# Splitting each row gather and scatter of a mixture-of-experts kernel in two, and moving a wait and the routing of the last token tile

## The chip, the cores and the metric

One NeuronCore of one Trainium2 chip runs the whole program. The metric is device time in microseconds (us) of one execution. The kernel before takes 714.67 us, the median of three runs (713.92 to 717.95).

## The reference, cut to what matters

One layer works on 512 tokens of width 1024. A token mixer comes first (one combined projection, four branches, sigmoid gates, an output projection), then a mixture of experts, then a last RMSNorm. What the change touches is the mixture:

```python
g_idx = jnp.argmax(group_probs, axis=-1)                 # 1 of 4 groups
top_p, top_i = lax.top_k(jax.nn.softmax(in_group), 2)    # 2 of its 8 experts
expert_id = g_idx[:, None] * 8 + top_i
for e in range(32):
    hid = jax.nn.silu(t @ w_expert_gate[e]) * (t @ w_expert_up[e])
    out = out + combine[:, e:e + 1] * (hid @ w_expert_down[e])
```

Each token goes to two of 32 experts, so there are 1024 token rows to gather and as many result rows to put back. The weights of all the experts, 96 matrices of 1 MB, are read once. The reference's routing on its own inputs gives the experts 0 to 31 these numbers of tokens:

```
6 30 32 38 12 22 2 4 64 60 45 26 52 49 28 16 35 31 47 33 34 32 49 11 23 34 56 19 25 14 30 65
```

## The kernel before, in words

**Mixer.** TensorE works through eleven slices of the combined projection (the last is `fk`, the keys of the forgetting attention), then through sixteen steps of attention, into which the first gate products are woven by `gates(count)`. Ahead of the first gate products TensorE waits until all six attention slices have been taken out of PSUM (`evacuated`, L1822 and on). `fk` sits in banks 4 and 5; the first 24 gate products write bank 6 and the six branch products behind them write bank 4.

**Output projection and routing.** The output projection runs over two halves of the columns, b = 0 and 1, and four tiles of 128 tokens each (L2008). VectorE adds each result to the residual (`residual`, L1114), TensorE transposes the sum (L1957), ScalarE copies it out of PSUM (L1000), and TensorE forms the router logits (`router_logits`, L1967). VectorE then picks the group and the two experts in a chain of small dependent instructions (`route`), TensorE counts the earlier tokens of each expert (`rank_products`, L1978), and VectorE makes two one-hot matrices: `chosen`, which picks the rows of expert pair 0, and `hot`, which makes the table of slots. `choose_rows` (L2014) multiplies `chosen` with the tokens, so pair 0 needs no gather. Its two PSUM banks are copied out, one by ScalarE (L1020) and one by VectorE (L1442). `first_table` (L2031, L1986) makes the table.

**Expert turns.** Experts are worked in pairs, each with 64 slots: the even expert of a pair has partitions 0 to 63, the odd one 64 to 127. There are 17 turns. Turns 0 to 6 are pairs 0 to 6. Turn 7 (`OVER`) is the fullest expert alone, its tokens over 64 in the second half; turn 8 (`PART`) is its partner alone in the first half. Turns 9 to 15 are pairs 8 to 14, and turn 16 is pair 7, in the place of the pair that was taken apart; the results of turns 15 and 16 stay on the chip and are not scattered. A turn is: gate and up matmuls (L2155), transposes of the next turn's gathered rows `xg` (L2121), transposes of the hidden values (L2164), down matmuls (L2181), then ScalarE and VectorE each copy half of the result to the one buffer `ye` (L1059, L1652), which may be done only when the scatter of the turn before has landed.

**Queues.** GpSimd issues one indirect gather per turn (L726, `xg` from `x2_dram`, rows by `toks`) and one indirect scatter (L733, `ye` to `y_dram`, rows by `slots`). Both have 128 rows; those of turn 8 have 64. An empty slot holds an index that is out of bounds, and its row is not moved. SyncE issues the weights in a fixed order into a ring of 21 units of 1 MB (L521), each as soon as the unit that held its place has been used: a gate unit frees with `g_done`, an up unit with `gu_done`, a down unit with `y_ps`. When the scatters have landed it issues the loads of the result rows of token tile 1 (L600), the last two weight units, and the other result rows. VectorE adds up the rows of tile 1 ahead of the hidden values of the last turn (`gather_results`, L1093), and the last norm follows.

**Places of slots.** `slot_no` says which of an expert's tokens a partition holds. Partition 32a + 4b + d of a half holds the tokens 32a + 8d to 32a + 8d + 7, forwards or backwards over b = 0 to 7.

Of the kernel before, what the change touches and what calls it, by code (L numbers as in the profile page):

```python
# [48 lines left out]
def hybrid_trunk(nc, x, mix_norm_g, w_in, b_forget, conv_a_w, conf_dw_w, conf_dw_b, conf_ln_g,  # L49
                 conf_ln_b, w_branch, w_gate, b_gate, w_out, ffn_norm_g, w_router_group,  # L50
                 w_router_expert, w_expert_gate, w_expert_up, w_expert_down, final_norm_g, out):
    P = 128
# [50 lines left out]
    with main:  # L103
# [182 lines left out]
        toks = sb(moe, "toks", [NPAIR + 1], I32)  # L286
        cw_diag = sb(moe, "cw_diag", [2, P])
# [119 lines left out]
        FIXED = 4  # L407
        LAST = NPAIR
# [14 lines left out]

        def halves(row):

            return row.rearrange("p (b n) -> p b n", b=2)

# [51 lines left out]
        def _(sp_e):  # L479
# [94 lines left out]
            for t in range(NT):  # L574
                sp_e.wait_ge(S["x2_ready"], NT + t + 1)
# [26 lines left out]
            for s in range(2):  # L602
                sp_e.wait_ge(scattered[s], 16 * (NPAIR // 2 - s))
# [16 lines left out]
            with sp_e.If(most > SLOT):  # L620
                sp_e.wait_ge(S["out_done"], 16 * NT)
                with sp_e.Fori(1, PASSES) as c:

                    sp_e.wait_ge(S["y_ps"], c * (2 * NPAIR) + 2)
                    sp_e.wait_ge(S["rank_ready"], NT)
                    for w in range(NPAIR * UPP):
                        if w >= NUP:
                            wait_reuse(c, w)
                        load_unit_no(w, c)
                for s in range(2):  # L630
                    sp_e.wait_ge(scattered[s], 16 * (NPAIR // 2 * PASSES - s))
# [7 lines left out]
        def _(pool):  # L639
# [79 lines left out]
            def rows_of(c, i):  # L719

                return slice(0, SLOT if isinstance(c, int) and i == PART else P)

            def gather(c, i, s):

                n, p = rows_of(c, i), column(c, i)
                pool.indirect_dma_start(out=xg[n, s, :], out_offset=None, in_=x2_dram[:, :],  # L726
                                        in_offset=bass.IndirectOffsetOnAxis(ap=toks[n, p], axis=0),
                                        bounds_check=last_token, oob_is_err=False).then_inc(g_full[s], 16)

            def scatter(c, i, s):  # L730

                n, p = rows_of(c, i), column(c, i)
                pool.indirect_dma_start(out=y_dram[:, :], out_offset=bass.IndirectOffsetOnAxis(ap=slots[n, p], axis=0),  # L733
                                        in_=ye[n, :], in_offset=None, bounds_check=last_row,
                                        oob_is_err=False).then_inc(scattered[s], 16)

            def expert_pass(c):
# [3 lines left out]
                pool.wait_ge(S["idx_ready"], c + 1)  # L741
# [40 lines left out]
        def _(act):  # L782
# [213 lines left out]
            def router_input(n):  # L996

                b, t = n // NT, n % NT
                act.wait_ge(S["xt2_ps"], n + 1)
                act.activation(xt2[:, t % 2, b * (KC // 2):(b + 1) * (KC // 2), :], bank[4 + n % 2][:, :].rearrange("p (c s) -> p c s", s=P),  # L1000
                               ACT.Copy).then_inc(S["moved_a"], 1)

            def token_squares(n):

                b, t = n // NT, n % NT
                act.wait_ge(S["x2_ready"], n + 1)
# [12 lines left out]
            act.wait_ge(S["routed_ps"], NT + 1)  # L1019
            act.activation(xg[:, 0, 0:T], bank[0][:, :], ACT.Copy).then_inc(S["moved_a"], 1)  # L1020
# [8 lines left out]
            def expert_pass(c):  # L1029

                first = c if isinstance(c, int) else 1
                for i in range(NPAIR + 1 if isinstance(c, int) else NPAIR):
# [19 lines left out]
                    else:  # L1052

                        if not isinstance(c, int):
                            act.wait_ge(scattered[1 - s], c * (NPAIR // 2 * 16) + ((i - 1) // 2 + s) * 16)
                        elif i:
                            act.wait_ge(scattered[1 - s], ((i - 1) // 2 + 1) * 16)
# [31 lines left out]
        def _(dve):  # L1089
# [18 lines left out]
            def residual(t, b):  # L1108
# [4 lines left out]
                half = x2[:, t, b * T:(b + 1) * T]  # L1113
                dve.tensor_tensor(half, half, bank[t][:, :], ALU.add).then_inc(S["x2_ready"], 1)  # L1114
# [251 lines left out]
            def route(t):  # L1366
# [10 lines left out]
                st.link(stt(re[:, 2, :], ro[:, 0, t, :], 2 * FAR, re[:, 0, :], ALU.mult, ALU.add))  # L1377
                yield
                first_max(re[:, 2, :], NE, rs[:, 3, t:t + 1], re[:, 3, :], best)
                st.mark(dve.tensor_scalar(rg[:, 0, t, :], gl, top, None, ALU.subtract))  # L1380
                dve.wait_ge(S["m_ready"], 2 * t)
                stt(rmask[:, t, :], re[:, 3, :], best, ro[:, 0, t, :], ALU.is_equal, ALU.add).then_inc(S["m_ready"], 1)
                dve.tensor_scalar(ro[:, 1, t, :], re[:, 3, :], best, None, ALU.is_equal).then_inc(S["m_ready"], 1)
                dve.wait_ge(S["m_ready"], 2 * t + 2)
                for j in range(2):
                    st.mark(dve.tensor_scalar(rv[:, t, j, :], ro[:, j, t, :], row_no[:, t, j:j + 1], None, ALU.mult))
                yield
# [46 lines left out]
            dve.wait_ge(S["sq_done"], 3 * NT)  # L1434
            dve.reduce_sum(stat[:, 0, :], sq_part[:, :, :], AX.X).then_inc(S["sq2_sum"], 1)
            for part in range(2):
                next(routes[NT - 1])
            choose(NT - 1)
            rank_tokens(NT - 2)
            rank_tokens(NT - 1)  # L1440
            dve.wait_ge(S["routed_ps"], NT + 2)
            dve.tensor_copy(xg[:, 0, T:2 * T], bank[1][:, :]).then_inc(S["hot_ready"], 1)  # L1442

            def slot_columns(n, found):

                table = found[:, 256:256 + NE].rearrange("p (e h) -> p h e", h=2)
                for h in range(2):
                    half = slice(h * SLOT, (h + 1) * SLOT)
                    dve.tensor_scalar(slots[half, 0:NPAIR], table[half, h, :], float(UNUSED), None, ALU.add).then_inc(S["slots_in"], 1)
                dve.wait_ge(S["slots_in"], n)  # L1450
                dve.tensor_scalar(toks[:, 0:NPAIR], slots[:, 0:NPAIR], 1, None, ALU.arith_shift_right).then_inc(S["idx_ready"], 1)

# [52 lines left out]
            def exchange_columns():  # L1505
# [6 lines left out]
                st.link(dve.tensor_copy(slots[:, FIXED:NPAIR], slot_f[:, FIXED:NPAIR]))  # L1512
                one_column(bank[7][:, 256:256 + NE], emask)
# [21 lines left out]
            def overflow_column():  # L1535

                second = slice(SLOT, P)
# [3 lines left out]
                st.link(dve.tensor_scalar(slots[second, NPAIR:NPAIR + 1], rs[second, 13, 0:1], float(UNUSED), None, ALU.add))  # L1541
# [4 lines left out]
            def first_exponents():  # L1546

                st.link(dve.tensor_tensor(rg[:, 2, :, :], rg[:, 0, :, :], stat[:, 2, :].unsqueeze(2).to_broadcast([P, NT, NG]), ALU.mult))
# [46 lines left out]
            def expert_pass(c):  # L1595
# [5 lines left out]
                if isinstance(c, int):  # L1601
                    dve.wait_ge(S["slot_ps"], 1)
                    slot_columns(2, bank[3])
# [8 lines left out]
                for i in range(turns):  # L1612
# [32 lines left out]
                    else:  # L1645

                        if not isinstance(c, int):
                            dve.wait_ge(scattered[1 - s], c * (NPAIR // 2 * 16) + ((i - 1) // 2 + s) * 16)
                        elif i:
                            dve.wait_ge(scattered[1 - s], ((i - 1) // 2 + 1) * 16)  # L1650
# [32 lines left out]
            with dve.If(most[0] > SLOT):  # L1683
# [20 lines left out]
                with dve.Fori(1, PASSES) as c:  # L1704

                    for s in range(2):
                        dve.wait_ge(scattered[s], c * (NPAIR // 2 * 16) - s * 16)
# [3 lines left out]
                    slot_columns(c * 2 + 2, bank[7])  # L1711
# [12 lines left out]
        def _(pe):  # L1724
# [90 lines left out]
            for name in ("sq", "sk", "sv", "fq", "fk", "fv"):  # L1815
# [55 lines left out]
            gates(PER_TILE)  # L1871
# [77 lines left out]
            def router_transposes(n):  # L1949
# [5 lines left out]
                for c in range(KC // 2):  # L1955
                    d = (b * (KC // 2) + c) * P
                    last = nc.tensor.transpose(bank[4 + n % 2][:, c * P:(c + 1) * P], x2[:, t, d:d + P], ident[:, :])  # L1957
                last.then_inc(S["xt2_ps"], 1)

            def router_logits(n):  # L1960

                b, t = n // NT, n % NT
                pe.wait_ge(S["moved_a"], n + 1)
                if b and t:
                    pe.wait_ge(S["m_ready"], 2 * t - 1)
                for c in range(b * (KC // 2), (b + 1) * (KC // 2)):
                    last = nc.tensor.matmul(bank[6][:, t * NR:(t + 1) * NR], xt2[:, t % 2, c, :], wr[:, c, :],  # L1967
                                            start=c == 0 and t == 0, stop=c == KC - 1, skip_group_check=True)
# [67 lines left out]

            first_table()
# [25 lines left out]
            def table_products(i, k):  # L2063
# [9 lines left out]
                if i == SPILL and k == 0:  # L2073
                    pe.wait_ge(S["hot_ready"], ALL_HITS + 2)
# [38 lines left out]
            def x_transposes(c, i, s, b):  # L2113

                if isinstance(c, int) and i == 0:
                    pe.wait_ge(S["moved_a"], 2 * NT + 1)
                    pe.wait_ge(S["hot_ready"], ALL_HITS + 1)
                elif b == 0:
                    pe.wait_ge(g_full[s], (i + 1) // 2 * 16 if isinstance(c, int) else c * (NPAIR // 2 * 16) + (i // 2 + 1) * 16)
# [5 lines left out]
            def expert_pass(c):  # L2125
# [69 lines left out]
            with pe.If(most > SLOT):  # L2195
                pe.wait_ge(S["rank_ready"], NT)
                with pe.Fori(1, PASSES) as c:
                    pe.wait_ge(S["hot_ready"], c + (ALL_HITS + 2))
# [30 lines left out]
```

## Time and profile before

| | |
|---|---|
| median of three runs | 714.67 us |
| the profiled execution | 714.88 us |
| its span, first to last instruction | 712.9 us |
| around the span | 2.0 us |
| granted TensorE clock, mean | 0.997 |
| TensorE matmul busy | 690.4 us, 97% of the span |
| VectorE, ScalarE, GpSimd busy | 372.7, 254.7, 80.0 us |
| bytes moved by DMA | 164.57 MB, mean 231 GB/s |

The page and the answers of the trace give the time of each instruction, what ended the idle time before it, and how busy the 16 DMA engines of the core were. "DMA share" is the mean busy share of these 16, so a share near 0.5 may be eight engines busy and eight idle. Share and GB/s can differ: an engine whose packets take long is busy and moves little.

### The profile page before, as it was taken

What the parts mean: (1) busy time and instruction counts of PE and PEld (TensorE: products, weight loads), DVE (VectorE), ACT (ScalarE), POOL (GpSimd) and SP (SyncE); (2) the same over time, 40 slices, a digit from 0 to 9 for tenths busy, and PEclk for the clock granted to TensorE, in tenths of its full rate; (3) what the DMA queues carried; (4) which work ended last, traced back from release to release, by engine and by line L of the source; (5) the groups of instructions that cost most, each with busy time, mean ns of one, the idle gap of its engine ahead of it and who ended that gap; (6) DMA issues with size and microseconds to landing.
All of it is one profiled execution on the core that took longest, in us unless ns stands there. A gap on an engine that the chain in (4) does not pass through costs nothing.

```text
span 712.9 us, 10002 instructions
## 1 busy us (share of the span) xinstructions
PE 690.4 (97%) x3923; PEld 507.5 (71%) x3923; DVE 372.7 (52%) x725; ACT 254.7 (36%) x423; POOL 80.0 (11%) x116
## 2 busy tenths in 40 slices
PE   7999999999999999999999999999999999999794
PEld 6888988777777777788888888665555556555442
DVE  5378996667676868656446214852423221212227
ACT  7332134577676777544243211210111111111113
POOL 2000922000000101100003000011111112121000
PEclk9999999999999999999999999999999999999998
DMA  7523144322222111493406699699999999999983
GB/s 241 176 63 116 61 126 147 134 74 75 74 74 68 46 60 53 161 384 114 135 2 236 239 376 348 268 353 394 399 417 421 403 420 419 418 418 418 420 353 130
DMA packets 60360, 164.57 MB, mean 231 GB/s; under 512 B 7866, under 2 KB 39687, under 8 KB 47892
## 3 DMA queue, kind: packets, MB, share of 16 engines
q1 hardware_dynamic: 54820, 151.77, 56.1%
q0 software_dynamic: 5488, 12.11, 4.5%
q8 instruction: 33, 0.54, 0.3%
q14 instruction: 19, 0.16, 0.1%
HBM read 155.68 MB, written 16.00 MB: 241 GB/s over the span
## 4 chain that ended last, share of the span: by engine, by line
PE 90%; DMA 4%; DVE 4%; ACT 1%; issue 1%; SPq 0%; POOLq 0%; DVEq 0%; ACTq 0%
PE psum L1731 31%; PE psum L2155 15%; PE psum L1830 12%; PE psum L2181 8%; PE psum L2008 6%; PE psum L1842 3%; PE psum L2121 2%; DMA ring_e<-y_dram 2%; DVE ring_e L1093 2%; PE psum L1855 1%; PE psum L1884 1%; DMA y_dram<-ye,slots 1%; PE psum L2164 1%; PE psum L1967 1%; PE psum L1919 1%; PE psum L1907 1%
## 5 line engine op out<-in xcount | busy, mean ns | idle before, releaser
L1731 PE MATMUL psum<-xh,wh 128*128 128x512 f32 x256 | 99.9, 390 | 0.8 <-DVE xl L1093 0.8
L1731 PE MATMUL psum<-xl,wh 128*128 128x512 f32 x256 | 99.6, 389 | 0.0
L1731 PE MATMUL psum<-xh,wl 128*128 128x512 f32 x256 | 99.6, 389 | 0.0
L1096 DVE TENSOR_TENSOR wl<-raw,wh 128x1280 fp32r<-128x1280 f32 (+4 forms) x37 | 71.8, 1946 | 24.8 <-ACT wh L789 9.0
L1093 DVE SCALAR_TENSOR_TENSOR hid<-psum,rslot,act_g 128x256 f32<-128x256 f32 x17 | 8.2, 484 | 95.1 <-PE psum L2155 94.6
L1731 PEld LDWEIGHTS psum<-xh,wh 128*128 128x128 f32 x256 | 48.1, 188 | 11.1 <-DVE xl L1093 1.0
L1731 PEld LDWEIGHTS psum<-xh,wl 128*128 128x128 f32 x256 | 48.1, 188 | 9.9
L1731 PEld LDWEIGHTS psum<-xl,wh 128*128 128x128 f32 x256 | 48.1, 188 | 9.8
L1830 PE MATMUL psum<-xh,wh 128*128 128x512 f32 x128 | 51.3, 401 | 1.3 <-DVE k_fl L1093 1.3
L1830 PE MATMUL psum<-xh,wl 128*128 128x512 f32 x128 | 50.1, 391 | 0.0
L1830 PE MATMUL psum<-xl,wh 128*128 128x512 f32 x128 | 49.9, 390 | 0.0
L1093 DVE SCALAR_TENSOR_TENSOR sg<-cu,ch,sg 128x512 f32<-128x512 f32 x60 | 48.8, 886 | 0.0
L2155 PE MATMUL psum<-ring_w,xT 128*64 128x256 f32 x256 | 38.8, 383 | 0.0
L1042 ACT ACTIVATE act_g<-psum,rslot 128x256 f32<-128x256 f32 x17 | 8.1, 474 | 80.2 <-PE psum L2155 60.7
L1044 ACT ACTIVATE hidT<-psum 128x256 f32<-128x256 f32 x17 | 6.5, 384 | 78.4 <-PE psum L2164 78.4
L1652 DVE COPY ye<-psum 128x512 f32<-128x512 f32 x15 | 10.4, 692 | 44.2 <-PE psum L2181 44.2
L733 POOL DMA_INDIRECT y_dram<-ye,slots x15 | 15.1, 1007 | 158.1 <-DVE ye L1652 114.5
L1323 DVE TENSOR_TENSOR gp<-gs,psum 128x512 f32<-128x512 f32 x16 | 11.0, 687 | 36.4 <-PE psum L1731 35.6
L2155 PEld LDWEIGHTS psum<-ring_w,xT 128*64 128x64 f32 x256 | 22.4, 136 | 10.5 <-issue 3.4
L964 ACT ACTIVATE gs<-psum,bg 128x512 f32<-128x512 f32 x16 | 10.9, 687 | 49.8 <-PE psum L1731 49.7
L1830 PEld LDWEIGHTS psum<-xh,wh 128*128 128x128 f32 x128 | 24.1, 188 | 6.2 <-issue 1.7
L1830 PEld LDWEIGHTS psum<-xh,wl 128*128 128x128 f32 x128 | 24.0, 188 | 5.2
(383 smaller groups left out, 1517.1 us busy)
## 6 DMA issues: line engine op xcount, KB each, us to landing
raw<-in_w_gate SPq DMA_DIRECT2D x16, 1024.0 KB, 6.4
raw<-in_w_in SPq DMA_DIRECT2D x9, 1024.0 KB, 5.5
ring_w<-in_w_expert_gate SPq DMA_DIRECT2D x8, 1024.0 KB, 20.4
ring_w<-in_w_expert_up SPq DMA_DIRECT2D x8, 1024.0 KB, 17.1
ring_h<-in_w_expert_down SPq DMA_DIRECT2D x8, 1024.0 KB
ring_h<-in_w_expert_gate SPq DMA_DIRECT2D x6, 1024.0 KB
ring_e<-in_w_expert_down SPq DMA_DIRECT2D x6, 1024.0 KB, 17.7
ring_e<-in_w_expert_gate SPq DMA_DIRECT2D x6, 1024.0 KB, 22.5
```

The lines of the kernel that those rows point to most:

```text
L733: pool.indirect_dma_start(out=y_dram[:, :], out_offset=bass.IndirectOffsetOnAxis(ap=slots[n, p], axis=0), in_=ye[n, :], in_offset=None, bo ...
L964: act.activation(gs[:, m, :], gate_bank(cg, m)[:, :], ACT.Sigmoid, bias=bg[:, d:d + 1]).then_inc(S["gate_mul"], 1)
L1093: return dve.scalar_tensor_tensor(out=out_, in0=a, scalar=s, in1=b, op0=o0, op1=o1)
L1096: return dve.tensor_tensor(dst, src, hi.bitcast(F32), ALU.subtract)
L1323: dve.tensor_tensor(gp[:, m, :], gs[:, m, :], branch_bank(cg, m)[:, :], ALU.mult).then_inc(S["gate_free"], 1)
L1731: last = nc.tensor.matmul(dst, a, b, start=start and n == 0, stop=stop and n == len(seq) - 1)
L1830: last = nc.tensor.matmul(bank[6 + n % 2][:, :], a[:, c, f], b[:, c, :], start=c == 0 and q == 0, stop=c == KC - 1 and q == 2)
L1842: last = nc.tensor.matmul(bank[4 + n % 2][:, :], a[:, j, f], b[g][:, j, :], start=j == 0 and q == 0, stop=j == BJ - 1 and q == 2)
L2008: last = nc.tensor.matmul(bank[t][:, :], x_[:, t, c, :], w_[:, b, c, :], start=c == 0 and m == 0, stop=c == KC - 1 and m == 2)
L2121: last = nc.tensor.transpose(bank[b][:, (k % 4) * P:(k % 4 + 1) * P], xg[:, s, :].rearrange("p (n c) -> p c n", c=KC)[:, k, :], ident[:, :])
L2155: last = nc.tensor.matmul(dst[half, 0:FE], xT[:, k, half], w[h][:, k, :], start=k == 0, stop=k == KC - 1)
L2181: last = nc.tensor.matmul(bank[5 + b][half, :], hidT[:, m, half], w_d[h][:, m, b * T:(b + 1) * T], start=m == 0, stop=m == FE // P - 1)
```

## The change

1. Every gather and every scatter is two: one for partitions 0 to 63 and one for 64 to 127, each with 64 rows. Two new columns, `slots_b` and `toks_b`, hold the indices of the second half in partitions 0 to 63. Semaphore counts double (`HALVES`), less 16 behind turn 8, which has one half only.
2. The order of `slot_no` changes: the eight-token groups k = 0 to 3 sit at d = 0, 2, 3, 1 for a = 0 and at d = 2, 0, 1, 3 for a = 1.
3. The wait for `fk` stands behind the first 24 gate products.
4. The last token tile's second half is added, transposed, copied and multiplied in two parts of 256 columns (`blocks_of`).
5. In `route`, two instructions move from the second part to the first; `rg` is no longer made per tile but once in `first_exponents`; the row values of the last two tiles and the sum of squares come later (`row_values`). `choose_rows(0, 1)` goes behind the last logits.
6. ScalarE copies both banks of pair 0, and `first_table` goes behind the transposes of pair 0.

```diff
+        HALVES = 2 * 16
+        def blocks_of(n):
+            return (slice(0, KC // 4), slice(KC // 4, KC // 2)) if n == 2 * NT - 1 else (slice(0, KC // 2),)
+        def one_less(s, i=PART):
+            return 16 if s == PART % 2 and i >= PART else 0
...
             def gather(c, i, s):
-                n, p = rows_of(c, i), column(c, i)
-                pool.indirect_dma_start(out=xg[n, s, :], out_offset=None, in_=x2_dram[:, :],
-                                        in_offset=bass.IndirectOffsetOnAxis(ap=toks[n, p], axis=0),
+                p = column(c, i)
+                pool.indirect_dma_start(out=xg[first, s, :], out_offset=None, in_=x2_dram[:, :],
+                                        in_offset=bass.IndirectOffsetOnAxis(ap=toks[first, p], axis=0),
                                         bounds_check=last_token, oob_is_err=False).then_inc(g_full[s], 16)
+                if whole(c, i):
+                    pool.indirect_dma_start(out=xg[second, s, :], out_offset=None, in_=x2_dram[:, :],
+                                            in_offset=bass.IndirectOffsetOnAxis(ap=toks_b[first, p], axis=0),
+                                            bounds_check=last_token, oob_is_err=False).then_inc(g_full[s], 16)
...
-                    for d in range(4):
-                        base, step = SLOT // 2 * a + 8 * d, 1
-                        if d % 2:
+                    for k, d in enumerate((2, 0, 1, 3) if a else (0, 2, 3, 1)):
+                        base, step = SLOT // 2 * a + 8 * k, 1
+                        if k % 2:
...
-                dve.tensor_tensor(half, half, bank[t][:, :], ALU.add).then_inc(S["x2_ready"], 1)
+                for part in (slice(0, T // 2), slice(T // 2, T)) if b and t == NT - 1 else (slice(0, T),):
+                    half = x2[:, t, b * T:(b + 1) * T][:, part]
+                    dve.tensor_tensor(half, half, bank[t][:, part], ALU.add).then_inc(S["x2_ready"], 1)
...
             for n in range(2 * NT):
                 router_input(n)
                 token_squares(n)
+            for b in range(2):
+                act.wait_ge(S["routed_ps"], NT + b + 1)
+                act.activation(xg[:, 0, b * T:(b + 1) * T], bank[b][:, :], ACT.Copy).then_inc(S["moved_a"], 1)
...
-            for name in ("sq", "sk", "sv", "fq", "fk", "fv"):
+            for name in ("sq", "sk", "sv", "fq", "fv"):
                 evacuated(pe, name)
...
-            gates(PER_TILE)
+            gates(BEHIND_SCORES)
+            evacuated(pe, "fk")
+            gates(PER_TILE - BEHIND_SCORES)
...
             router_transposes(2 * NT - 1)
-            choose_rows(0, 1)
             rank_products(NT - 2)
             router_logits(2 * NT - 1)
+            choose_rows(0, 1)
...
-            first_table()
...
                 for b in range(2):
                     x_transposes(c, 0, first % 2, b)
+                if isinstance(c, int):
+                    first_table()
```

## Rows read from the trace of the kernel before

**Rows 1.** The chain that ended last (start us, us, what), from turn 13.
```profile
643.51 3.65 PE psum L2181 x16
...
655.70 3.68 PE psum L2181 x16
659.47 0.70 DVE ye L1652
...
660.99 8.79 DMA y_dram<-ye,slots
670.17 14.43 DMA ring_e<-y_dram
684.63 1.30 DVE ring_e L1093
```

**Rows 2.** Stretches of the run, with DMA share and GB/s at the end of each row.
```profile
454.00:690.00 236.00, 228.09 (x1597) 132.85 (x1595) 69.53 (x206) 30.02 (x60) 31.27 (x31) 1.00 1.01 407
468.00:470.00 2.00, 2.00 (x22) 1.61 (x20) 1.77 (x12) 1.26 (x1) 1.10 (x2) 1.00 0.81 264
```

**Rows 3.** Who TensorE waited for, from 655 to 690 us.
```profile
PE psum L2155 <- DMA ring_x<-in_w_expert_up: 1.6, 1, 1.6
```

**Rows 4.** Stretches at the end of the DMA work.
```profile
688.00:689.00 1.00, 1.00 (x6) 0.87 (x7) 0.00 (x0) 0.39 (x1) 0.00 (x0) 1.00 1.05 426
692.00:693.00 1.00, 1.00 (x8) 0.29 (x5) 0.20 (x1) 0.69 (x1) 0.00 (x0) 1.00 0.52 213
689.00:698.00 9.00, 9.00 (x34) 3.94 (x33) 4.17 (x5) 2.66 (x3) 0.00 (x0) 1.00 0.44 178
```

**Rows 5.** DMA queue of the gathers and scatters: packets, MB, share; 505 to 685 us.
```profile
q0 software_dynamic: 3707, 7.09, 10.4%
```

**Rows 6.** The same queue, 1.1 us of turn 7's scatter (579.7), then of turn 8's (591.75).
```profile
q0 software_dynamic: 40, 0.07, 17.5%
...
q0 software_dynamic: 37, 0.12, 27.7%
```

**Rows 7.** Stretches around turn 8's gather, issued at 552.54.
```profile
505.00:557.00 52.00, 51.85 (x382) 29.73 (x380) 14.06 (x39) 5.75 (x12) 8.03 (x8) 1.00 1.02 420
559.00:560.00 1.00, 1.00 (x8) 0.37 (x6) 0.00 (x0) 0.00 (x0) 0.00 (x0) 1.00 1.03 254
560.00:561.00 1.00, 1.00 (x8) 0.35 (x6) 0.00 (x0) 0.42 (x1) 0.00 (x0) 1.00 0.97 332
561.00:562.00 1.00, 1.00 (x8) 0.43 (x6) 0.08 (x1) 0.18 (x1) 0.00 (x0) 1.00 1.01 393
```

**Rows 8.** Instructions in order of time: projection end, routing of the last tile, turn 0.
```profile
138.88 0.47 PE L1830 MATMUL psum<-xh,wh 128*128 128x512 f32 x1 [1.32 <-DVE k_fl L1093]
...
454.94 1.06 PE L1967 MATMUL psum<-wr,xt 128*128 128x36 f32 x8
...
455.84 3.68 PE L2014 MATMUL psum<-x,chosen 128*128 128x512 f32 x8
...
459.58 0.24 PE L1978 MATMUL psum<-rmask,oneb 128*128 128x32 bf16 x3
...
462.59 1.04 PE L1986 MATMUL psum<-rv,hot 128*128 128x32 f32 x8
...
463.52 1.13 PE L2121 MATMUL psum<-ident,xg 128*128 128x128 f32 x8
...
465.16 3.67 PE L2155 MATMUL psum<-ring_z,xT 128*64 128x256 f32 x32 [0.51 <-DVE xT L1463]
```

**Rows 9.** A usual turn: scatter, the two copies waiting for it, its issue to landing.
```profile
612.21 1.00 POOL L733 DMA_INDIRECT y_dram<-ye,slots  x1 [9.87 <-DVE ye L1652]
...
621.16 0.60 ACT L1059 ACTIVATE ye<-psum 128x512 f32<-128x512 f32 x1 [2.10 <-PE psum L2181]
622.88 0.69 DVE L1652 COPY ye<-psum 128x512 f32<-128x512 f32 x1 [3.07 <-PE psum L2181]
...
DMA to landing us min/median/max: 8.5/8.5/8.5
```

More of the change, by code:

```diff
@@ L286, in hybrid_trunk @@
         toks = sb(moe, "toks", [NPAIR + 1], I32)
+        slots_b = sb(moe, "slots_b", [NPAIR + 1], I32)
+        toks_b = sb(moe, "toks_b", [NPAIR + 1], I32)
         cw_diag = sb(moe, "cw_diag", [2, P])
@@ L574, in _ @@
             for t in range(NT):
-                sp_e.wait_ge(S["x2_ready"], NT + t + 1)
+                sp_e.wait_ge(S["x2_ready"], NT + t + 1 if t < NT - 1 else 2 * NT + 1)
                 sp_e.dma_start(x2_dram[t * P:(t + 1) * P, :], x2[:, t, :]).then_inc(S["x2_out"], 16)
@@ L998, in router_input @@
                 b, t = n // NT, n % NT
-                act.wait_ge(S["xt2_ps"], n + 1)
-                act.activation(xt2[:, t % 2, b * (KC // 2):(b + 1) * (KC // 2), :], bank[4 + n % 2][:, :].rearrange("p (c s) -> p c s", s=P),
-                               ACT.Copy).then_inc(S["moved_a"], 1)
+                for k, part in enumerate(blocks_of(n)):
+                    act.wait_ge(S["xt2_ps"], n + k + 1)
+                    act.activation(xt2[:, t % 2, b * (KC // 2):(b + 1) * (KC // 2), :][:, part, :],
+                                   bank[4 + (n + k) % 2][:, :].rearrange("p (c s) -> p c s", s=P)[:, part, :], ACT.Copy).then_inc(S["moved_a"], 1)
             def token_squares(n):
                 b, t = n // NT, n % NT
-                act.wait_ge(S["x2_ready"], n + 1)
+                act.wait_ge(S["x2_ready"], n + 1 if n < 2 * NT - 1 else 2 * NT + 1)
                 if n:
@@ L1438, in _ @@
             choose(NT - 1)
+            for t in (NT - 2, NT - 1):
+                row_values(t)
             rank_tokens(NT - 2)
             rank_tokens(NT - 1)
-            dve.wait_ge(S["routed_ps"], NT + 2)
-            dve.tensor_copy(xg[:, 0, T:2 * T], bank[1][:, :]).then_inc(S["hot_ready"], 1)
+            dve.wait_ge(S["sq_done"], 3 * NT)
+            dve.reduce_sum(stat[:, 0, :], sq_part[:, :, :], AX.X).then_inc(S["sq2_sum"], 1)
             def slot_columns(n, found):
@@ L1512, in exchange_columns @@
                 st.link(dve.tensor_copy(slots[:, FIXED:NPAIR], slot_f[:, FIXED:NPAIR]))
+                st.link(dve.tensor_copy(slot_f[first, :], slots_b[first, 0:NPAIR]))
+                exchanged(moved[first, :], slot_f[first, :], slot_f[first, OVER:OVER + 1], gap[first, :])
+                st.link(dve.tensor_copy(slots_b[first, FIXED:NPAIR], slot_f[first, FIXED:NPAIR]))
+                st.mark(dve.tensor_scalar(toks_b[first, FIXED:NPAIR], slots_b[first, FIXED:NPAIR], 1, None, ALU.arith_shift_right))
                 one_column(bank[7][:, 256:256 + NE], emask)
@@ L1535, in overflow_column @@
             def overflow_column():
-                second = slice(SLOT, P)
+                first, second = slice(0, SLOT), slice(SLOT, P)
                 dve.wait_ge(S["slot_ps"], 3)
@@ L1540, in overflow_column @@
                 one_column(bank[7][:, 256:256 + NE], fmask)
-                st.link(dve.tensor_scalar(slots[second, NPAIR:NPAIR + 1], rs[second, 13, 0:1], float(UNUSED), None, ALU.add))
+                st.mark(dve.tensor_scalar(slots[second, NPAIR:NPAIR + 1], rs[second, 13, 0:1], float(UNUSED), None, ALU.add))
+                st.link(dve.tensor_scalar(slots_b[first, NPAIR:NPAIR + 1], rs[first, 13, 0:1], float(UNUSED), None, ALU.add))
+                st.link(dve.tensor_scalar(toks_b[first, NPAIR:NPAIR + 1], slots_b[first, NPAIR:NPAIR + 1], 1, None, ALU.arith_shift_right))
                 dve.tensor_scalar(toks[:, NPAIR:NPAIR + 1], slots[:, NPAIR:NPAIR + 1], 1, None, ALU.arith_shift_right).then_inc(S["over_ready"], 1)
@@ L1954, in router_transposes @@
                     pe.wait_ge(S["moved_a"], n - 1)
[L1955 to L1958, printed above, removed]
+                for k, part in enumerate(blocks_of(n)):
+                    if k:
+                        pe.wait_ge(S["x2_ready"], n + k + 1)
+                        pe.wait_ge(S["moved_a"], n)
+                    for c in range(KC // 2)[part]:
+                        d = (b * (KC // 2) + c) * P
+                        last = nc.tensor.transpose(bank[4 + (n + k) % 2][:, c * P:(c + 1) * P], x2[:, t, d:d + P], ident[:, :])
+                    last.then_inc(S["xt2_ps"], 1)
             def router_logits(n):
                 b, t = n // NT, n % NT
-                pe.wait_ge(S["moved_a"], n + 1)
                 if b and t:
                     pe.wait_ge(S["m_ready"], 2 * t - 1)
-                for c in range(b * (KC // 2), (b + 1) * (KC // 2)):
-                    last = nc.tensor.matmul(bank[6][:, t * NR:(t + 1) * NR], xt2[:, t % 2, c, :], wr[:, c, :],
-                                            start=c == 0 and t == 0, stop=c == KC - 1, skip_group_check=True)
+                for k, part in enumerate(blocks_of(n)):
+                    pe.wait_ge(S["moved_a"], n + k + 1)
+                    for c in range(b * (KC // 2), (b + 1) * (KC // 2))[part]:
+                        last = nc.tensor.matmul(bank[6][:, t * NR:(t + 1) * NR], xt2[:, t % 2, c, :], wr[:, c, :],
+                                                start=c == 0 and t == 0, stop=c == KC - 1, skip_group_check=True)
                 if b:
```

63 lines of the change are left out of this document (35 added, 28 removed).

## The prediction

> **What bounds the kernel now.** I read the chain of waits first, then the DMA share by stretches, then who TensorE waits for. From 139 us to 459 us TensorE is never idle for long: the one stop by another engine is 1.32 us, ahead of the first gate product, until VectorE has taken `fk` out of PSUM [rows 8]. In the expert turns it is busy too, and this misleads: from 454 to 690 us the DMA engines have a share of 1.01 and move 407 GB/s [rows 2], while a turn eats six units, 6.3 MB, in 655.70 - 643.51 = 12.2 us [rows 1], which would be 516 GB/s. So the ring of 21 units runs empty, slowly, and by turn 15 TensorE waits for weights [rows 3]. The chain says the same: after turn 14 it goes through the last scatter, then 14.43 us of the load of the result rows, then VectorE [rows 1]. The DMA work from 454 us on is a fixed number of bytes, and the end is where it is done plus some 28 us of tail behind 684.63.
>
> **How it ends is the second thing to see.** At 688 us all engines are busy (1.05), at 692 the share is 0.52, and over the 9 us to 698 it is 0.44 [rows 4]. A mean engine is thus done at 689 + 9 x 0.44 = 693.0, the last at 698: some lag the mean by 5 us, and about half of them are late together. [...] In 1.1 us of turn 8's scatter, which has 64 rows and 30 tokens, 0.12 MB went; in as much time of turn 7's, which has 128 rows and its 65 tokens all but one in the first half, 0.07 MB [rows 6]. [...] The first halves hold much more: the even experts have 540 of the 1024 tokens, and turns 7 and 8 put 94 of their 95 in the first half. [...] A row costs an engine 0.104 x 180 us x 16 / (7.09 MB / 4096) = 0.173 us [rows 5]. [...]
>
> **The change part by part.** All in the profiled execution's own time, 714.88 us (712.9 of span and 2.0 around it); it lies 0.2 above the median of the runs.
>
> *The wait for `fk`.* The 1.32 us go. The 24 gate products now ahead of the wait are some 5 us of work (at most 24 x 0.47 [rows 8]) that need only the slices before, and VectorE is through with `fk` 1.3 us in. Nothing late comes next: up to 459 us TensorE has no second stop above 0.3 us. I take -1.3; the bounds are 0 (if ScalarE and VectorE set the pace of the attention steps) and -1.3.
>
> *The last tile's halves and the order of `route`.* Today the logits end at 456.00, four products of `choose_rows` fill TensorE to 459.52, and `rank_products` starts at 459.58 [rows 8], as VectorE's mask arrives. The halves bring the logits forward by some 0.6 us (one part's copy and products in place of two), and `route` gets 0.2 shorter, but `choose_rows(0, 1)`, 3.68 / 4 = 0.9 us, now stands behind the logits. So 455.4 + 5 x 0.86 = 459.7: the products now end last, and VectorE's gain is wasted. +0.1. If I mis-sized this by one such product, it is -0.8 to +0.2.
>
> *`first_table` behind the transposes.* Today it runs in the shadow of the two copies (1.04 us at 462.59, transposes from 463.52 [rows 8]). Then TensorE idles 0.51 us until VectorE has made the first half of `xT`. In the new order the transposes start at the same 463.5, since ScalarE makes both copies and the second one ends at 463.4; they end at 464.6, the table takes 1.3 us, and the gate products start at 465.9, not 465.16. +0.7. Bounds +0.2 and +1.1. Behind it the slots come 0.4 us later, and with two more small instructions the first gather 0.6; its landing has some 3 us to spare. SyncE's first refill waits for the gate products of turn 0 and is as late; the DMA engines are already short of work there (264 GB/s [rows 2]), so the 0.7 counts in full.
>
> *Two DMAs for one.* On GpSimd a turn has four issues of 1.3 us and not two, 5.2 of 12.2 us: nothing else is queued there. The second scatter is issued 1.3 us later. The scatter lands 8.5 us after its issue, at 620.7; ScalarE's copy wants it at 621.16 and VectorE's at 622.88 [rows 9]. ScalarE will be up to 1 us late, which nobody waits for, VectorE is in time. Cost 0, at most 0.5. VectorE's exchange in turn 2 is longer by about six small instructions, 1.2 us; the gather of turn 4 behind it has some 4 us to spare. 0.
>
> *The balance.* [...] It is a gain of 3.3 to 3.8; I take 3.3. [...] Bounds: 0 and -4.6.
>
> The sum: 714.9 - 1.3 + 0.1 + 0.7 - 3.3 = **711.1 us**.
>
> [...] In stretches of 1 us around turn 8's gather, the only gather before that has 64 rows, the rate falls from 420 to 254, 332 and 393 GB/s, at a full share [rows 7]; turn 8's scatter shows no such dip, and in 185 us there is no other. The shortfall is (166 + 88 + 27) KB / 420 GB/s = 0.67 us for 30 rows. [...]
>
> **The rivals.**
>
> *Narrow gathers choke (slower), 0.30.* Every gather becomes two like that of turn 8. The dip costs 0.67 us per 30 rows, and some 880 rows are gathered from turn 3 on: 19.7 us if each half pays in full. The second half follows 1.3 us behind and goes to the other 64 partitions, while the dip lasts 3 us, so about half may be saved: 9.8. The scatter's part of the balance (half of 3.3) stays. 714.9 - 0.5 - 1.6 + 9.8 = 722.6, up to 732 in full. It decides from 0.11 us per 30 rows on, where the loss eats the gain of 3.3 us; against it stands only that it is one event, seen alone and not with its other half beside it.
>
> *The halves don't even out (the change doesn't do what it says), 0.20.* [...] Then only the wait and the table count: 714.9 - 1.3 + 0.8 = 714.4. The same figure comes out if a mild choking, some 3 us, pays for the balance.
>
> **How the numbers follow.** The forecast has a chance of 0.50, with its own range 709.0 to 713.3 (balance by 4.6 and routing by -0.8 on one side, the wait lost on the other). No change that a measurement of this kernel can tell is within 0.5%, or 711.1 to 718.2 us: the forecast lies on its lower edge. So half of its chance is faster, with a little of the second rival: 0.29. The same: 0.25 + 0.16 = 0.41. Slower: 0.30. The range reaches from 709.0 to 724.5, which leaves out the full choking.
>
> **What would show it.** Right: no stop at the first gate product; gate products of turn 0 starting 0.7 us later than the rest of the shift; DMA share falling from 1 to 0 within 3 us, not 9; the rate between 505 and 650 us still near 420. Wrong: that rate at 400 or less with a full share, TensorE waiting for weights from turn 12 or 13 on; or a share near 0.5 for several us at the end as before.

## The result, and the profile after

The changed kernel takes 723.76 us (median of 4 runs, 722.86 to 724.27); the kernel before took 715.28 us beside it. The ratio is 1.0112, with a 95% interval of 1.008 to 1.0145: slower by 8.0 us (5.7 to 10.4), where I had forecast 3.8 us faster. The profiled execution took 722.86 us, its span is 721.1. The time is close to that of my first rival (722.6), to which I had given 0.30. Below, "faster by x us" is a ratio of runs of one session turned into us at 714.5, with its 95% interval in brackets; it can differ from the difference of the two medians by up to 1 us.

Stretches of the changed kernel (start and end, length, busy us of TensorE, its weight loads, VectorE, ScalarE, GpSimd, granted clock, DMA share, GB/s). The first row answers to [rows 2]; the last four are from two neighbouring turns:

```profile
454.00:690.00 236.00, 223.50 (x1540) 128.90 (x1539) 64.99 (x205) 28.87 (x57) 56.56 (x60) 0.99 1.01 386
505.00:685.00 180.00, 169.85 (x1173) 97.42 (x1170) 38.33 (x80) 20.27 (x41) 45.16 (x48) 0.98 1.02 385
522.00:529.00 7.00, 7.00 (x55) 4.26 (x51) 0.00 (x0) 0.47 (x1) 3.76 (x4) 0.93 1.01 413
529.00:535.00 6.00, 6.00 (x28) 3.60 (x27) 0.07 (x1) 0.00 (x0) 0.00 (x0) 0.51 1.02 301
535.00:545.00 10.00, 9.96 (x74) 5.61 (x75) 5.00 (x17) 1.45 (x3) 2.65 (x3) 1.00 1.01 418
545.00:550.00 5.00, 4.47 (x34) 2.68 (x32) 1.77 (x3) 0.38 (x1) 1.20 (x2) 1.00 1.01 420
```

The GpSimd issues whose rows move in those stretches (start, us, operation):

```profile
524.91 0.96 POOL L739 DMA_INDIRECT xg<-x_dram,toks  x1 [0.30 <-issue]
526.17 0.96 POOL L743 DMA_INDIRECT xg<-x_dram,toks_b  x1 [0.30 <-issue]
541.74 0.92 POOL L750 DMA_INDIRECT y_dram<-ye,slots  x1 [14.60 <-DVE ye L1692]
542.96 1.01 POOL L754 DMA_INDIRECT y_dram<-ye,slots_b  x1 [0.31 <-issue]
```

The share of the DMA engines is full in both kernels (1.01 and 1.02): by the share alone nothing has happened. What fell is what they move in that share, from 418 to 385 GB/s over 505 to 685 us. The engines aren't idle, their packets take longer: a packet of the weights' queue took 0.896 x 180 us x 16 / 8537 packets = 302 ns in this stretch, and 0.909 x 180 us x 16 / 9575 = 273 ns in the kernel before. The rate falls in bursts, one per turn, and from 665 to 685 us, behind the last gather (issued at 658.56), it is 415 again. The gathers issued at 524.91 and 526.17 move their rows from 529 to 535 us, and there the rate is 301 (414 in the same stretch of the kernel before). The scatters issued at 541.74 and 542.96 move theirs from 545 to 550 us, and there it is 420. TensorE's clock happens to be low in that one burst (0.51). It isn't the cause: in the split alone (below) the same burst has a clock of 1.00 and 327 GB/s:

```profile
529.00:535.00 6.00, 5.96 (x42) 3.76 (x43) 1.61 (x3) 0.38 (x1) 0.00 (x0) 1.00 1.03 327
```

Who TensorE waited for in the changed kernel (us in total, times, longest), to be held against [rows 3]:

```profile
PE psum L2210 <- DVE hid L1116: 6.5, 11, 1.6
...
PE psum L2201 <- DMA ring_x<-in_w_expert_up: 1.8, 1, 1.8
...
PE psum L2227 <- DMA ring_q<-in_w_expert_down: 0.8, 1, 0.8
PE psum L2201 <- DMA ring_e<-in_w_expert_up: 0.7, 1, 0.7
```

Its waits for `hid`, the hidden values that VectorE makes, have grown too. In the kernel before they were:

```profile
PE psum L2164 <- DVE hid L1093: 2.0, 2, 1.7
```

The chain that ended last, from turn 13 on, which answers to [rows 1]:

```profile
630.40 32.96 DMA ring_q<-in_w_expert_down
663.49 3.67 PE psum L2227 x16
667.25 0.70 DVE ye L1692
...
669.98 8.13 DMA y_dram<-ye,slots_b
678.51 14.27 DMA ring_e<-y_dram
692.80 1.30 DVE ring_e L1116
```

Its first row is what the chain before did not have: a step that waits for a weight unit. The 33 us from issue to landing are not new in themselves, since one unit (`ring_p`, 33.0 us) took as long in the kernel before; new is that the products stand behind it. The last scattered turn's down products, which started at 655.70 [rows 1], start at 663.49.

The end of the DMA work, in stretches of 1 us, which answers to [rows 4]:

```profile
701.00:702.00 1.00, 1.00 (x7) 0.19 (x4) 0.72 (x1) 0.04 (x1) 0.00 (x0) 1.00 1.01 401
702.00:703.00 1.00, 1.00 (x3) 0.52 (x4) 0.32 (x1) 0.98 (x2) 0.00 (x0) 1.00 0.90 360
703.00:704.00 1.00, 1.00 (x3) 0.38 (x2) 1.00 (x2) 0.95 (x1) 0.00 (x0) 1.00 0.73 295
704.00:705.00 1.00, 1.00 (x5) 0.42 (x3) 0.96 (x2) 0.00 (x0) 0.00 (x0) 1.00 0.44 176
705.00:706.00 1.00, 1.00 (x5) 0.67 (x4) 0.96 (x2) 0.00 (x0) 0.00 (x0) 1.00 0.18 74
```

The shares from 701 us on add up to 3.3, so a mean engine is done at 704.3 and the last at 706: the lag is 1.7 us, where it was 5. In this execution the balance came as forecast, and the sum closes: the mean engine is done 704.3 - 693.0 = 11.3 us later, the lag is 3.3 smaller, together 8.0; the span grew by 721.1 - 712.9 = 8.2.

### The profile page after: what moved, and what is told of

Its sections match the earlier page's. It is cut to its first block, busy times and chain, and to the rows that moved or that the text cites. A ratio compares the mean times of both kernels' runs of the same rounds, so it can differ in the third digit from the quotient of the medians.

```text
span 721.1 us, 10044 instructions
## 1 busy us (share of the span) xinstructions
PE 694.0 (96%) x3923; PEld 509.4 (71%) x3923; DVE 372.1 (52%) x732; ACT 255.1 (35%) x425; POOL 105.3 (15%) x145
## 4 chain that ended last, share of the span: by engine, by line
PE 81%; DMA 8%; DVE 4%; SPq 4%; ACT 1%; issue 1%; POOL 0%; POOLq 0%; DVEq 0%; ACTq 0%
PE psum L1771 30%; PE psum L1870 12%; PE psum L2201 9%; PE psum L2055 6%; PE psum L2227 6%; DMA ring_q<-in_w_expert_down 5%; SPq L532 4%; PE psum L1882 3%; DMA ring_e<-y_dram 2%; DVE ring_e L1116 2%; PE psum L1895 1%; PE psum L1926 1%; PE psum L2165 1%; DMA y_dram<-ye,slots_b 1%; PE psum L2061 1%
## 5 line engine op out<-in xcount | busy, mean ns | idle before, releaser
L1771 PEld LDWEIGHTS psum<-xh,wh 128*128 128x128 f32 x256 | 48.0, 188 | 11.1 <-DVE xl L1116 1.0
L1771 PEld LDWEIGHTS psum<-xl,wh 128*128 128x128 f32 x256 | 48.1, 188 | 9.8
L2201 PE MATMUL psum<-ring_w,xT 128*64 128x256 f32 x256 | 41.0, 393 | 0.0
L1692 DVE COPY ye<-psum 128x512 f32<-128x512 f32 x15 | 10.4, 692 | 45.0 <-PE psum L2227 45.0
L1870 PEld LDWEIGHTS psum<-xl,wh 128*128 128x128 f32 x128 | 24.1, 188 | 4.6
```

The lines of the kernel that those rows point to most:

```text
L1771: last = nc.tensor.matmul(dst, a, b, start=start and n == 0, stop=stop and n == len(seq) - 1)
L1870: last = nc.tensor.matmul(bank[6 + n % 2][:, :], a[:, c, f], b[:, c, :], start=c == 0 and q == 0, stop=c == KC - 1 and q == 2)
L2201: last = nc.tensor.matmul(dst[half, 0:FE], xT[:, k, half], w[h][:, k, :], start=k == 0, stop=k == KC - 1)
```

## The experiments

The theory now (A): a gather that writes 64 rows into one half of the partitions slows whatever else the DMA engines move. The rate of 385.2 instead of 417.5 GB/s over 180 us is a loss of 32.3 / 417.5 x 180 = 13.9 us. The rivals: the number of DMAs and of GpSimd's issues (B), and the rest of the change (C). Four kernels each take back one part.

**Whole gathers.** Edit, and the wait counts to match:

```
-    out=xg[first, s, :] ... ap=toks[first, p]     and the second gather
+    n = slice(0, P) if whole(c, i) else first
+    out=xg[n, s, :] ... ap=toks[n, p]
```

Turn 8's gather, which fills one half only, stays at 64 rows.

> The changed kernel with one gather DMA of 128 rows per turn instead of two of 64; the scatters stay in two halves, and the new order of the places stays. Theory A (choking: a gather whose 64 rows land in partitions 0 to 63 or 64 to 127 only slows every other transfer while it runs): the rate between 505 and 685 us goes back to 415 to 420 GB/s. The choking was worth 8.5 (measured loss) + 1.3 (fk) + 3.3 (balance) = 13 us, and all of it goes; what is left is the wait for fk, -1.3, and the scatters' part of the balance, which by the count of rows per engine takes the lag from 4.6 to 3.0 us, -1.5. Expected: 2.8 us faster than before, 712. Theory B (it is the number of DMAs and of GpSimd issues, four per turn and not two, so gathers and scatters hurt alike): half of the loss stays, 3 to 5 us slower than before, and the rate dips at the scatters as well.

Measured: 711.15 us beside 714.07, ratio 0.995 (0.993 to 0.9969), faster by 3.6 us (2.2 to 5.0). A holds in size, B falls. This is also the shortest way from the changed kernel: only the gathers differ (and with them one issue per turn), the medians are 12.6 us apart, and by the shares at the end a mean engine is done at 690.8 and not at 704.3, 13.5 us earlier. A's 13.9 lie near both.

**Whole scatters,** the same edit in `scatter`, gathers in halves.

> The changed kernel with one scatter DMA of 128 rows per turn; the gathers stay in two halves of 64. Theory A: the scatters had no part in the loss and lose only their share of the balance (lag by the count of rows: 1.1 in the changed kernel, 2.7 here), so 8.5 + 1.6 = 10 us slower than before, rate in 505 to 685 us near 390 GB/s as in the changed kernel. Theory B (number of DMAs): about 3 to 5 us slower than before, like the kernel with whole gathers.

Measured: 724.26 us, ratio 1.0129 (1.0106 to 1.0151), slower by 9.2 us; 383 GB/s. GpSimd has three issues here and three in the kernel with whole gathers, and 13 us lie between the two.

**Both whole.**

> The changed kernel with both gather and scatter as one DMA of 128 rows; all the rest of the change stays (fk wait moved, the last token tile's halves, the table behind the transposes, the longer index work on VectorE). Theory A: the loss is in the gathers alone, so this is 1.3 us faster than before (fk), with the last engines idle from 689 to 698 us as before. My prediction's sizes for the rest, +0.1 for the routing and +0.7 for the table, would make it -0.5. Theory C (the harm comes from the later first gather and the longer index work, with TensorE starved in turns 2 to 4): still slower than before by 3 us or more.

Measured: 713.22 us, ratio 0.9984 (0.9967 to 1.0002), faster by 1.1 us (-0.1 to 2.4). C falls: without the split nothing in the change costs time that can be told. Between the two kernels with whole gathers, the split scatters give 3.6 - 1.1 = 2.5 us; both intervals are some 2.5 us wide.

**The split alone,** put into the kernel before.

> The kernel before with only the split: gathers and scatters in two halves, the second half's index columns, and the new order of the places; the fk wait, the routing and the table are as before. Theory A: choking of 13 us less 3.3 of balance: 9.8 us slower than before. Theory C (the rest of the change does part of the harm): 5 us or less slower than before.

Measured: 726.09 us, ratio 1.0157 (1.0133 to 1.0181), slower by 11.2 us (9.5 to 12.9). The 9.8 expected is inside.

The rows of 505 to 685 us show which part carries the loss. Whole gathers; whole scatters; both whole; the split alone:

```profile
505.00:685.00 180.00, 177.00 (x1249) 101.57 (x1246) 43.22 (x85) 21.16 (x43) 35.02 (x37) 1.00 1.02 418
```

```profile
505.00:685.00 180.00, 168.67 (x1166) 98.15 (x1164) 38.05 (x78) 19.51 (x40) 34.85 (x36) 0.98 1.02 383
```

```profile
505.00:685.00 180.00, 175.84 (x1242) 100.74 (x1238) 42.52 (x84) 20.74 (x42) 25.10 (x25) 1.00 1.02 417
```

```profile
505.00:685.00 180.00, 167.53 (x1170) 97.49 (x1172) 39.36 (x80) 19.28 (x40) 45.19 (x48) 0.99 1.02 385
```

Share 1.02 in all four; 418 and 417 GB/s with gathers of 128 rows, 383 and 385 with gathers of 64. The scatters make no difference to the rate that exceeds 2 GB/s.

**The wait for `fk` alone.**

```
-    for name in ("sq", "sk", "sv", "fq", "fk", "fv"):
+    for name in ("sq", "sk", "sv", "fq", "fv"):
...
-    gates(PER_TILE)
+    gates(BEHIND_SCORES)
+    evacuated(pe, "fk")
+    gates(PER_TILE - BEHIND_SCORES)
```

> The kernel before with nothing but the wait for fk moved behind the first 24 gate products. My term: 1.3 us faster. If ScalarE and VectorE set the pace of the attention steps (the other bound): no difference. Set against the kernel without a split (0.85 us faster than before, interval -0.2 to 2.4), it prices the routing and the table together: I expect +0.1 to +0.8 for these two, so this kernel a little faster than that one.

Measured: 713.37 us, ratio 0.998 (0.9966 to 0.9994), faster by 1.4 us (0.4 to 2.4).

**The wait and the split scatters, without the routing and the table.**

> The kernel before with the moved wait for fk, the scatters in two halves and the new order of the places; gathers whole, routing and table as before. Theory A: -1.3 for fk and -1.5 for the scatters' balance, 2.8 us faster than before, the same as the kernel with whole gathers (2.9 measured). If the last tile's halves, the route order and the table are worth something of their own (my sizes: +0.1 and +0.7, by the trace of the changed kernel +0.1 in all), this one differs from that by as much: -0.8 to -0.1 us. Theory D (routing is worth 1 to 2 us in itself, as the 12.0 us loss of the split alone beside 9.2 of the whole change might say): this one is 1 to 2 us slower than the kernel with whole gathers.

Measured: 712.0 us, ratio 0.9953 (0.9935 to 0.9971), faster by 3.4 us (2.1 to 4.6), for 3.6 with routing and table. These two are worth nothing that can be told; D (they are worth 1 to 2 us) falls.

**The old places,** in the kernel with whole gathers: `for k, d in enumerate((0, 1, 2, 3))`.

> The kernel with whole gathers and split scatters, with the old order of the places. [...]

Measured: 712.91 us, ratio 0.9977 (0.9961 to 0.9994), faster than before by 1.6 us, so 2.0 slower than with the new places (711.15 us); the intervals, of two sessions, overlap a little. I had expected 1.7 slower, an estimate from an assumed way of dealing rows to engines. The end of the DMA work speaks too. New places, with the mean engine done at 690.8 and the last by 694, then old, at 691.0 and by 696 to 697:

```profile
692.00:693.00 1.00, 1.00 (x4) 0.38 (x2) 0.96 (x2) 0.00 (x0) 0.00 (x0) 1.00 0.13 53
```

```profile
692.00:693.00 1.00, 1.00 (x4) 0.49 (x3) 0.03 (x2) 0.73 (x2) 0.00 (x0) 1.00 0.24 98
693.00:694.00 1.00, 1.00 (x4) 0.42 (x3) 1.00 (x2) 1.00 (x1) 0.00 (x0) 1.00 0.19 78
694.00:695.00 1.00, 1.00 (x4) 0.52 (x3) 0.96 (x2) 0.24 (x1) 0.00 (x0) 1.00 0.15 61
```

With the old places a few engines (0.19 of 16 is three) go on for two more us. The lag is 5 to 6 us with the old places and 3.2 with the new ones, at 417 and 418 GB/s over 505 to 685 us: the order of the places sets a part of the lag and leaves the rate alone. Which engine moves the row of which partition no run shows.

**Interleaved gathers.** Two gathers of 64 rows as in the changed kernel, but one writes the even and one the odd partitions:

```
-    out=xg[first, s, :] ...
+    n = slice(0, P, 2) if whole(c, i) else first
+    out=xg[n, s, :] ...
...
-    out=xg[second, s, :] ...
+    out=xg[1::2, s, :] ...
```

> The changed kernel whose two gather DMAs of 64 rows write every second partition, one the even and one the odd ones, instead of partitions 0 to 63 and 64 to 127; count of DMAs, rows, indices and bytes is the same. This changes what is computed: the rows of an expert no longer stand in its own half, so tokens meet the wrong expert's weights; the amount of work stays. Theory A (what chokes is that all sixteen engines write into one half of the partitions): no choking, rate in 505 to 685 us back at 417 GB/s, about 710 to 713. Theory G (what chokes is any gather of 64 rows dealt over sixteen engines, such as its reads of the token rows from DRAM): as the changed kernel, 723 to 724, rate 385 GB/s.

```profile
505.00:665.00 160.00, 154.48 (x1093) 88.18 (x1094) 35.91 (x75) 18.04 (x37) 43.02 (x46) 1.00 1.02 417
665.00:685.00 20.00, 19.96 (x142) 11.07 (x140) 5.18 (x9) 2.71 (x5) 1.83 (x2) 1.00 0.91 370
```

The rate is 417 GB/s until 665 us (381 in the changed kernel): with the same DMAs, rows and indices, but every second partition as the target, the choking is gone. So a gather of 64 rows as such doesn't choke (G falls); the same rows choke when they go into one half of the partitions, 381 against 417 GB/s, which is A. How many engines take part in either kind of gather no run shows. Should their number differ, that may be the reason behind A.

The time, though, is 713.83 us, ratio 0.9996 (0.9977 to 1.0015), 3.3 short of the kernel with whole gathers, and I had expected 710 to 713. TensorE waits there for no weights, but 6.7 us for `hid`. From 665 to 685 us the share itself falls, to 0.91: the engines run short of work, which is another thing than choking. That asked for two more kernels.

**Interleaved gathers, whole scatters,** so that GpSimd issues three DMAs per turn.

> The kernel with the two gathers on even and odd partitions, now with one scatter DMA of 128 rows: GpSimd has three issues per turn, not four, and the second gather is issued 1.2 us earlier. As there, an expert's rows stand in other places than its weights want, so what is computed is changed, and the amount of work is not. The kernel with four issues had no choking (412 GB/s) but was only 1 us faster than before, and there VectorE's product hid started 0.5 to 0.7 us after the last gate/up product in 10 turns of 16 instead of 0.12, which held TensorE up for 6.4 us. Theory H (the fourth issue of GpSimd falls into the moment of hid and holds it up): here hid is late in at most 3 turns, TensorE waits for it 2 to 3 us in all, and the kernel is about 1 to 2 us faster than that one although the scatters' balance is lost. Theory I (the lateness has to do with the interleaved or split gathers themselves): hid is late in about 10 turns as there.

**Whole gathers and an empty one:** the second gather has 64 indices out of bounds and a target of one element.

> The kernel with whole gathers and split scatters (711.15 us, 2.9 faster than before) with a second gather DMA per turn that moves nothing: all its 64 indices are out of bounds. GpSimd has four issues per turn again, at the same places as in the changed kernel, and no narrow row is written but those of turn 8. Theory A and H: rate in 505 to 685 us 417 GB/s, but hid late by 0.5 us in 10 or so turns, TensorE held up 6 us by it in place of 2.6, and since TensorE is then hardly ever short of weights, 1.5 to 3 us slower than the kernel with whole gathers, some 713 to 714. Theory A without H: as that kernel, 711.2. If issues and descriptors of narrow gathers made the 13 us (theory B): 718 or more.

TensorE's waits for `hid`: interleaved; interleaved with whole scatters; whole gathers with an empty one; whole gathers alone; and the split alone in the kernel before:

```profile
PE psum L2211 <- DVE hid L1117: 6.7, 12, 0.9
```

```profile
PE psum L2208 <- DVE hid L1114: 3.0, 4, 1.7
```

```profile
PE psum L2215 <- DVE hid L1121: 6.7, 12, 1.0
```

```profile
PE psum L2207 <- DVE hid L1113: 2.9, 4, 1.7
```

```profile
PE psum L2189 <- DVE hid L1110: 2.3, 2, 1.7
```

In three kernels with four issues per turn (the changed kernel, the interleaved gathers and the empty one) VectorE starts `hid` about 0.6 us late in some ten turns; with three issues it does not. The empty gather ran at 413 GB/s (416 until 665 us), so it choked nothing, but took 716.59 us, ratio 1.0022 (1.0004 to 1.004): 5.2 us slower than the kernel with whole gathers, more than the 1.5 to 3 expected. Its 11 runs lie in two groups, four at 713.5 to 713.7 and seven at 716.4 and more; the profile is of the first, which is 2.4 us slower than the kernel with whole gathers, as expected. What makes the second is open. The kernel with three issues and interleaved gathers had punctual `hid` but no gain: 714.58 us, ratio 1.0004 (0.999 to 1.0018), where I had expected 1 to 2 us less than with four. It has lost the scatters' balance, and TensorE waits for weights again (2.1 us). And the last row is an exception: the split alone has four issues too, at the same place in the turn, and `hid` is punctual. So the lateness was seen only with a fourth issue, but the fourth issue does not do it alone; what else it takes was not found.

**Turn 8's gather with 128 rows,** in the kernel with whole gathers: `n = slice(0, P)`.

> The kernel with whole gathers and split scatters in which turn 8's gather, the last narrow one, is of 128 rows too; its second half fetches the rows of another expert (about 16) that nothing uses. Theory A: the dip at 558 to 562 us, worth 0.67 us, is gone and the rate stays at 417 to 420 there; the 16 rows more cost eight engines 2 x 0.173 = 0.35 us. So 0.3 us faster than the kernel with whole gathers, which the times can hardly tell; the rate of the stretch is what counts. Rival: the dip belongs to turn 8 itself (the exchange of the experts) and not to the gather's 64 rows: it stays.

Around that gather, with 64 rows and then with 128:

```profile
558.00:559.00 1.00, 1.00 (x8) 0.31 (x6) 0.10 (x1) 0.00 (x0) 0.00 (x0) 1.00 1.13 377
559.00:560.00 1.00, 1.00 (x6) 0.29 (x4) 0.00 (x0) 0.00 (x0) 0.00 (x0) 1.00 0.96 307
```

```profile
558.00:559.00 1.00, 1.00 (x6) 0.29 (x4) 0.01 (x1) 0.00 (x0) 0.00 (x0) 1.00 1.02 422
559.00:560.00 1.00, 1.00 (x8) 0.35 (x6) 0.00 (x0) 0.32 (x1) 0.00 (x0) 1.00 1.05 426
```

The dip belongs to the gather. It also shows how little one event tells of the size: against 420 GB/s the 64 rows cost (43 + 113 + 6) KB / 420 GB/s = 0.39 us from 558 to 561 us here (414 GB/s in the third), where the same gather cost 0.67 in the kernel before. 710.89 us, ratio 0.9948 (0.9932 to 0.9964), the fastest kernel here, by no more than can be told from the one with whole gathers. The 0.35 us that I expected for the 16 rows more took them as shared by eight engines, which no run shows; these times can't tell.

**First halves only.**

> The kernel with whole gathers and split scatters in which each gather fetches only its first 64 rows, into partitions 0 to 63; the second halves are not fetched, so part of the input of the experts is left out. It tells whether the two narrow gathers of a turn choke together or each for itself. The changed kernel lost 13.9 us in 505 to 685 us (rate 385.2 for 417.5) with some 830 rows gathered in it, 0.50 us per 30 rows; turn 8 alone had 0.67. If each half pays in full and for itself (0.50 per 30 rows): some 510 rows of first halves, 8.5 us lost, rate near 398 GB/s. If two halves beside each other save half (my assumption): one alone pays 0.67 or more per 30 rows, 11 us lost, rate near 392 GB/s.

```profile
505.00:685.00 180.00, 174.88 (x1220) 100.42 (x1217) 39.90 (x82) 20.77 (x42) 34.11 (x37) 0.99 1.02 398
```

398 GB/s is a loss of 8.5 us. Counted again, 552 rows of first halves are gathered in this stretch and 326 of second halves: 0.46 us per 30 rows alone, and 13.9 us for 878, 0.47 per 30, with both. Nothing is saved by two halves beside each other. The kernel takes 715.68 us, ratio 1.0009 (0.9988 to 1.0031): 326 of 878 rows left out, and still 4 us slower than the kernel that fetches all in whole gathers.

## Why the prediction was wrong, step by step

- **The step that failed** is the one from the dip to the sum: I had read rightly that the one narrow gather costs 0.67 us at a full DMA share [rows 7], and then left that out of the sum. The forecast's sum took the gathers' choking as zero, with 0.50 against 0.30 for the rival, on the ground that it was one event. It was a fact about every gather into one half of the partitions, not about that turn: at 0.47 us per 30 rows it is four times the 0.11 from which the rival decides. The term of the sum that stood at 0 measured 13.9 us, and the forecast's own sign of being wrong came, 382 GB/s from 505 to 650 us at a share of 1.02.
- **The rival's time was right in part by luck.** Its mechanism held, its price did not: 9.8 us with half saved and 19.7 in full, for the measured 13.9. Two errors partly cancel: nothing is saved, and a row costs 0.47 / 0.67 of what turn 8's showed. Beside it the rival allowed 0.5 + 1.6 us for gains that came to 1.4 + 3.3. With the measured terms the sum is 714.9 - 1.4 - 3.3 + 13.9 = 724.1; the profiled execution took 722.9. The 1.2 us between are unexplained, and within what the runs can tell.
- **The wait for `fk`** was right: the first gate product starts at 137.44 us with no stop, for 138.88 [rows 8], and alone it is worth 1.4 us (1.3 forecast).
- **The last tile's halves and the route order** were right at nothing. The first of `rank_products` starts at 458.05, for 459.58 [rows 8]: 1.5 earlier, which is the `fk` wait's gain and nothing more.
- **`first_table` behind the transposes** was mis-sized: 0.0 in place of +0.7. In the changed kernel:

```profile
461.67 1.16 PE L2165 MATMUL psum<-ident,xg 128*128 128x128 f32 x8 [0.69 <-ACT xg L1040]
...
462.67 0.25 PE L2078 MATMUL psum<-rmask,oneb 128*128 128x32 bf16 x4
...
462.77 1.04 PE L2033 MATMUL psum<-rv,hot 128*128 128x32 f32 x8
...
463.75 3.67 PE L2201 MATMUL psum<-ring_z,xT 128*64 128x256 f32 x32
```

  The gate products start at 463.75, for 465.16 [rows 8]: 1.4 earlier, no less than the rest. I had held the transposes at 463.5, but they start at 461.67, 1.85 earlier, 0.4 of it their own. The last four products of `choose_rows` start at 459.00, for 460.67, which is 0.2 of it; the second copy, now ScalarE's, takes 0.60 us for VectorE's 0.69; and the transposes no longer queue behind the table. With the 0.51 us in which TensorE idled before, that pays for the table's 1.1 us.
- **Two DMAs for one** at nothing was wrong in a way that the changed kernel hides. The second scatter of turn 14 lands 8.1 us after its issue, and TensorE waits for neither of the two copies behind them, as forecast. But the fourth issue goes with a late `hid`, 6.5 us of TensorE's time in all for 2.0 before. While the DMA engines set the pace it costs little (the split alone has no late `hid` and is no faster); with the choking gone it comes to the front.
- **The balance** came, and its size is less sure than one number makes it look. The 3.3 us of the sum, the 1.5 and 1.6 that the expectations give the scatters' part, and their lags of 1.1 to 4.6 us are estimates from a count of rows per engine, which no run shows; [rows 6] show what two scatters moved in 1.1 us, not by which engines. What the runs showed in its place are the lags at the end: by the shares the lag falls by 3.3 us in the changed kernel and by 2.3 in the split alone; the split scatters by themselves take it from 4.3 to 3.2 us, and by the times they give 2.5. With the old places it is 5 to 6 us.

## What to carry to other kernels

Where a trace shows one event of the kind that a change will repeat in every turn, multiply it before anything else: a dip of 0.67 us, repeated, was the whole result, though one event gave its size no better than 0.39 to 0.67. Look at GB/s beside the DMA share; choking was seen only there. In this kernel it paid to split the indirect DMAs that read the on-chip memory (2.5 us), and to keep those that write it at 128 partitions (12.6 us).

## What the runs showed of the hardware

- Scatters of 64 rows from one half of the partitions cost the other transfers nothing (420 GB/s from 545 to 550 us in the changed kernel), gathers of 64 rows into one half do (301 from 529 to 535 us).
- In the turns of five of the fourteen profiled executions TensorE's granted clock was low for 3 to 7 us, in no fixed place: 0.51 from 529 to 535 us in the changed kernel, behind 7 us in which it was busy throughout, and 0.50 from 643 to 646 in the kernel with whole scatters. In the kernel with `fk` and split scatters it is 0.51 from 488 to 494 us, and 0.50 again from 532 to 538; the profiled execution took 715.44 us there, and the other five 709.8 to 712.2:

```profile
488.00:494.00 6.00, 6.00 (x27) 3.48 (x26) 0.00 (x0) 0.00 (x0) 0.00 (x0) 0.51 0.83 343
```

  The DMA share falls with it to 0.83, I take it because units of the ring come free later. In that kernel's second stretch, and in the changed kernel's, the share stays full (1.02), so there the fall will have cost little.
